# A gate table by expert, built by GpSimd's indirect adding DMAs into zeroed DRAM instead of by one-hot products on TensorE

## What is computed

```python
top_s, top_i = lax.top_k(sub_scores, K)                       # K = 16, 8 heads, 2 halves
cand_s = top_s[:, :, 0, :, None] + top_s[:, :, 1, None, :]
cand_id = top_i[:, :, 0, :, None] * N_KEYS + top_i[:, :, 1, None, :]
best_s, best_c = lax.top_k(cand_s.reshape(T, PEER_HEADS, K * K), K)
expert_id = jnp.take_along_axis(cand_id..., best_c, axis=-1)
gate = jax.nn.softmax(best_s, axis=-1)
a = jnp.einsum('pd,ped->pe', xb, expert_down[ids])
act = jax.nn.gelu(a, approximate=False) * gates
y = jnp.einsum('pe,ped->pd', act, expert_up[ids])
```

## Time and profile before

| | |
|---|---|
| median of 3 runs | 1516.51 us (1515.63 to 1518.48) |
| profiled execution, its own time | 1507.25 us |
| its span in the trace | 1505.4 us |
| busy: PE, DVE, ACT, POOL | 1386.3, 1022.5, 659.3, 50.7 us |
| mean granted clock of PE | 0.933 |

### The profile page before, as it was taken

One profiled execution on the slowest core, in us unless ns is written; L12 is line 12 of the kernel. 1 busy time (PEld: TensorE's weight loads), 2 busy tenths in 40 slices (PEclk: granted clock), 3 DMA queues, 4 the chain that ended last, 5 costly groups with the idle time before them and its releaser, 6 DMA issues.

```text
span 1505.4 us, 20658 instructions
## 1 busy us (share of the span) xinstructions
PE 1386.3 (92%) x8489; PEld 1235.0 (82%) x8489; DVE 1022.5 (68%) x1900; ACT 659.3 (44%) x853; POOL 50.7 (3%) x37
## 2 busy tenths in 40 slices
PE   2788987999999999999999999999799987799998
PEld 2576846999998999999888888888677976689987
DVE  5878746689999999844676676677646144545554
ACT  1445413454454444444545454454534144435443
POOL 0005000000000000000000000000001120000000
PEclk7788988999999999999999999999989555999999
DMA  9664444546655666768877887786535400425552
GB/s 365 229 223 148 150 151 157 187 176 236 240 194 214 249 252 252 277 259 330 301 275 279 292 290 288 269 315 235 189 126 184 141 1 1 167 101 180 198 194 84
DMA packets 118999, 316.05 MB, mean 210 GB/s; under 512 B 7662, under 2 KB 45807, under 8 KB 112506
## 3 DMA queue, kind: packets, MB, share of 16 engines
q1 hardware_dynamic: 105498, 263.35, 48.6%
q10 hardware_dynamic: 6912, 33.56, 5.6%
q0 software_dynamic: 6496, 17.84, 3.2%
HBM read 279.06 MB, written 34.60 MB: 208 GB/s over the span
## 4 chain that ended last, share of the span: by engine, by line
PE 82%; DVE 10%; DMA 3%; ACT 2%; issue 1%; SPq 1%; DVEq 0%; ACTq 0%
PE ps L621 10%; PE ps L620 10%; PE ps L619 10%; PE ps L607 10%; PE ps L609 9%; PE ps L608 9%; PE ps L816 4%; PE ps L597 3%; PE ps L599 3%; PE ps L598 3%; DVE w_lo L1376 2%; PE ps L866 2%; DMA arena<-in_ada_w 2%; PE ps L659 1%; PE ps L878 1%
## 5 line engine op out<-in xcount | busy, mean ns | idle before, releaser
L1376 DVE TENSOR_TENSOR w_lo<-wring,w_hi 128x1024 fp32r<-128x1024 f32 (+1 forms) x404 | 489.7, 1220 | 265.6 <-ACT w_hi L1017 264.1
L1017 ACT CAST w_hi<-wring 128x1024 fp32r<-128x1024 f32 (+1 forms) x404 | 420.3, 1045 | 389.0 <-PE ps L609 243.3
L607 PE MATMUL ps<-hT_hi,w_hi 128*128 128x256 f32 x1408 | 396.4, 282 | 15.3 <-DVE w_lo L1376 6.0
L608 PE MATMUL ps<-hT_lo,w_hi 128*128 128x256 f32 x1408 | 391.9, 278 | 0.0
L609 PE MATMUL ps<-hT_hi,w_lo 128*128 128x256 f32 x1408 | 391.7, 278 | 0.0
L607 PEld LDWEIGHTS ps<-hT_hi,w_hi 128*128 128x128 f32 x1408 | 266.8, 189 | 17.7 <-DVE hT_lo L1399 5.5
L608 PEld LDWEIGHTS ps<-hT_lo,w_hi 128*128 128x128 f32 x1408 | 267.1, 190 | 0.3
L609 PEld LDWEIGHTS ps<-hT_hi,w_lo 128*128 128x128 f32 x1408 | 266.9, 190 | 0.0
L621 PE MATMUL ps<-w_hi,a_lo 128*128 128x512 f32 x640 | 252.2, 394 | 0.0
L620 PE MATMUL ps<-w_lo,a_hi 128*128 128x512 f32 x640 | 250.9, 392 | 0.0
L619 PE MATMUL ps<-w_hi,a_hi 128*128 128x512 f32 x640 | 248.3, 388 | 0.0
(11 more groups left out here) (286 smaller groups left out, 1311.7 us busy)
## 6 DMA issues: line engine op xcount, KB each, us to landing
wring<-in_peer_down SPq DMA_DIRECT2D x32, 2048.0 KB, 8.6
wring<-in_peer_up SPq DMA_DIRECT2D x32, 2048.0 KB, 7.7
wring<-in_w_in SPq DMA_DIRECT2D x12, 2048.0 KB, 7.8
pages<-in_ada_w POOLq DMA_DIRECT2D x8, 2048.0 KB, 8.2
acts_by_expert<-pages ACTq DMA_DIRECT2D x32, 512.0 KB, 2.7
peer_arena<-gates_by_expert SPq DMA_DIRECT2D x16, 1024.0 KB, 11.0
peer_arena<-acts_by_expert SPq DMA_DIRECT2D x32, 512.0 KB, 8.5
wring<-in_w_up SPq DMA_DIRECT2D x8, 2048.0 KB, 8.3
```

Source lines behind the costliest of these rows:

```text
L607: pe.matmul(o, hi[:, k, :], hT_hi[:, k, :], start=(k == 0), stop=False)
L608: pe.matmul(o, hi[:, k, :], hT_lo[:, k, :], start=False, stop=False)
L1017: act.copy(split_part(kind, w_hi, u, width(kind, j)), part_of(kind, wring[:, n % RING, :], u, width(kind, j))).then_inc(split_hi, 1)
L1376: dve.tensor_tensor(lo, part_of(kind, wring[:, n % RING, :], u, width(kind, j)), hi, ALU.subtract)\
```

## The change

The table in DRAM becomes one flat array of 16384 x 256 numbers, expert by token. ACT zeroes it early in the program, in 8 DMAs of 2 MB from a zeroed piece of SBUF: 2 behind the split of win R_V, 3 behind that of wout 0, 3 behind that of wout 1. DVE works out place and gate of each choice head by head, in place of one batch behind the last head, with 10 `w_lo` parts per head instead of 6. For each head, rank (16) and token block (2), POOL issues one indirect DMA, which adds 128 gates, one per token, to 128 places of the table: 256 DMAs. Before it starts a head it waits until the adds of the head before it, for the same block, have landed. The one-hot rows, the transposes, the products, ACT's copies of them and its stores fall away. SP waits at the same place as before, now for the adds. ACT's softmax exponential comes once per head, not once for all.

```diff
@@ DMA of SP
-                sp.dma_start(gates_in[:, turn % 2, :, :, :].rearrange("p g f t -> p g (f t)"),
-                             gates_dram[:, :, turn * 2 * EF * 16:(turn + 1) * 2 * EF * 16].rearrange("g p n -> p g n"))\
+                rows = gates_dram[turn * 2 * CHUNK * T:(turn + 1) * 2 * CHUNK * T, :]
+                sp.dma_start(gates_in[:, turn % 2, :, :], rows.rearrange("(f p t) one -> p f (t one)", p=P, t=T))\
                     .then_inc(gates_landed[turn % 2], 16)
...
-            for u in range(2):
-                sp.wait_ge(gates_stored[u], 16 * (T // 32))
+            for b in range(NB):
+                sp.wait_ge(gates_added[b], 16 * PK * PH)
@@ PE
-            pe.wait_ge(S["sel_ready"], NB)
-            for b in range(NB):
-                for k in range(3):
-                    mm = pe.transpose(ps[:, 4 + b, k * P:(k + 1) * P], sel[:, b, k, :], ident)
...
-                    if 0 <= turn < T // TT:
-                        spread_products(turn)
@@ ACT
+            def fill_gates(turns):
+
+                act.wait_ge(S["zero_ready"], 1)
+                n = NE * T // FILLS
+                for turn in turns:
+                    act.dma_start(gates_dram[turn * n:(turn + 1) * n, :].rearrange("(r p n) one -> p r (n one)", p=P, n=ZEROS),
+                                  zeros.unsqueeze(1).to_broadcast([P, n // (P * ZEROS), ZEROS])).then_inc(gates_zeroed, 16)
...
+            fill_gates(range(0, 2))
...
+            fill_gates(range(2, 5))
...
+            fill_gates(range(5, FILLS))
...
+            def gate_exp(head):
+
+                act.wait_ge(S["score_max"], head + 1)
+                act.activation(gate_of[:, :, head, :], gate_of[:, :, head, :], ACT.Exp).then_inc(S["exp_done"], 1)
@@ POOL
+            pool.wait_ge(gates_zeroed, 16 * FILLS)
+            for head in range(PH):
+                pool.wait_ge(S["sel_ready"], head + 1)
+                for b in range(NB):
+                    if head:
+                        pool.wait_ge(gates_added[b], 16 * PK * head)
+                    for k in range(PK):
+                        pool.indirect_dma_start(gates_dram, bass.IndirectOffsetOnAxis(ap=place_of[:, b, head, k:k + 1], axis=0),
+                                                gate_of[:, b, head, k:k + 1], None, compute_op=ALU.add)\
+                            .then_inc(gates_added[b], 16)
@@ DVE
+                    if half == 0:
+                        if head:
+                            finish_gates(head - 1)
+                        next_rest()
+                        if head:
+                            tell("sel_ready")
...
+                for half in range(2):
+                    both(lambda b: dve.tensor_tensor(pick[:, half, b], bestf[:, b, half, head, :].unsqueeze(2)
+                                                     .to_broadcast([P, PK, PK]),
+                                                     con("iota")[:, 0:PK].unsqueeze(1).to_broadcast([P, PK, PK]), ALU.is_equal))
...
-            for q in range(T // OT):
...
-                for t in range(OT):
-                    at = q * OT + t
-                    first, second, weight = (selT[:, k, at:at + 1] for k in range(3))
-                    dve.tensor_scalar(onehot[:, q % OB, 0, t, :], con("iota"), first, None, ALU.is_equal)
-                    ins = dve.tensor_scalar(onehot[:, q % OB, 1, t, :], con("iota"), second, weight, ALU.is_equal, ALU.mult)
```

More of the change, by code:

```diff
@@ L120, in constants @@
     parts["iota"] = np.tile(np.arange(NKEY), (P, 1))
+    parts["token"] = i[:, None]
     at, out = 0, []
@@ L298, in two_blocks @@
         acts_in = [peer_arena[:, 8192 + k * 1024:9216 + k * 1024].rearrange("p (f t) -> p f t", f=EF) for k in range(AHEAD)]
[L299 to L300 removed]
+        pick = peer_arena[:, 12288:13312].rearrange("p (k b i j) -> p k b i j", k=2, b=NB, j=PK)
+        zeros = arena[:, 16000:16000 + ZEROS]
         cand, cand2 = (h_flat[:, k * 512:(k + 1) * 512].rearrange("p (b n) -> p b n", b=NB) for k in range(2))
@@ L363, in two_blocks @@
         S = {n: sem(n) for n in names}
-        gates_stored = [sem(f"gates_stored{k}") for k in range(2)]
+        gates_zeroed = sem("gates_zeroed")
+        gates_added = [sem(f"gates_added{k}") for k in range(NB)]
         gates_landed = [sem(f"gates_landed{k}") for k in range(2)]
@@ L798, in _ @@
             key_scores(3)
-            for j in range(1, TURN_AFTER + 1):
+            for j in range(1, STEPS):
                 by_columns("dn", j)
-            pe.wait_ge(S["sel_ready"], NB)
-            for b in range(NB):
-                for k in range(3):
-                    mm = pe.transpose(ps[:, 4 + b, k * P:(k + 1) * P], sel[:, b, k, :], ident)
[L806 to L813, removed]
-                    for t in range(OT):
[L815 to L826, removed]
-                    if 0 <= turn < T // TT:
-                        spread_products(turn)
-            pe.wait_ge(S["spread_out"], T // TT)
             for j in range(STEPS):
@@ L1167, in _ @@
                         split("ex", 0, acts_in[0], parts=[u])
[L1168 to L1174, removed]
+                    part = SPLIT_BEFORE[NTH["dn", j]] + PARTS + u - SPLIT_BEFORE[NTH["wq", 3]]
+                    if part % RESTS == 1 and 1 <= part // RESTS <= PH:
+                        gate_exp(part // RESTS - 1)
                 down_gelu(j)
@@ L1670, in top16, with tell, finish_gates @@
                 next_rest()
+            def tell(name):
+                both.settle()
+                dve.sem_inc(S[name], 1)
+            def finish_gates(head):
+                dve.wait_ge(S["exp_done"], head + 1)
+                both(lambda b: dve.tensor_reduce(gsum[:, b, head:head + 1], gate_of[:, b, head, :], AX.X, ALU.add))
+                both(lambda b: dve.reciprocal(gsum[:, b, head:head + 1], gsum[:, b, head:head + 1]))
+                both(lambda b: dve.tensor_scalar(gate_of[:, b, head, :], gate_of[:, b, head, :],
+                                                 gsum[:, b, head:head + 1], None, ALU.mult))
             for head in range(PH):
@@ L1683, in _ @@
                       lambda b: besti[:, b, 0, head, :])
[L1685 to L1688, removed]
-                    .then_inc(S["score_max"], 1)
-            both(lambda b: dve.tensor_copy(topf[:, b], topi[:, b]))
-            both(lambda b: dve.tensor_scalar(besti[:, b, 1, :, :], besti[:, b, 0, :, :], 15, None, ALU.bitwise_and))
@@ L1703, in _ @@
-            dve.wait_ge(S["exp_done"], 1)
-            both(lambda b: dve.tensor_reduce(gsum[:, b, :], gate[b], AX.X, ALU.add))
-            both(lambda b: dve.reciprocal(gsum[:, b, :], gsum[:, b, :]))
-            both.settle()
-            for b in range(NB):
-                dve.tensor_tensor(gate[b], gate[b], gsum[:, b, :].unsqueeze(2).to_broadcast([P, PH, PK]), ALU.mult)\
-                    .then_inc(S["sel_ready"], 1)
-            for u in range(PARTS):
-                next_rest()
-            dve.wait_ge(S["sel_turned"], 1)
@@ L1727, in _ @@
-            dve.sem_inc(S["late_free"], 1)
+                both(lambda b: dve.tensor_tensor(gate_of[:, b, head, :], best[:, b, head, :],
+                                                 best[:, b, head, 0:1].to_broadcast([P, PK]), ALU.subtract))
+                both(lambda b: dve.tensor_scalar(besti[:, b, 1, head, :], besti[:, b, 0, head, :], 15, None, ALU.bitwise_and))
+                tell("score_max")
+                both(lambda b: dve.tensor_scalar(besti[:, b, 0, head, :], besti[:, b, 0, head, :], 4, None,
+                                                 ALU.logical_shift_right))
@@ L1728, in _ @@
+                next_rest()
+            finish_gates(PH - 1)
+            next_rest()
+            tell("sel_ready")
             for n in range(next(placed), SPLIT_BEFORE[NTH["ex", 0]]):
```

75 lines of the change are left out of this document (24 added, 51 removed).

## The result

The changed kernel takes 1718.73 us (median of 4 runs, 1716.59 to 1722.66) against 1516.72 us before (4 runs beside it): ratio 1.1334, 95% interval 1.1308 to 1.1359. It is 202 us slower. I had forecast 1458 us, and a range up to 1590.

A forecast was written before the change was run, and what follows sets the result against it. PE was taken to set the pace, with DVE almost full. From 1505.4 us of span, less 73.6 removed, plus 3 (DVE) and 12 (fills), came 1446.8; against the median, 1458 us, range 1444 to 1590.

The forecast's parts named there:

- the price of an add: POOL's time for one of 256 adds: taken as 1.0 us, bounds 0.53 and 3.68, nothing late up to 1.04 us.
- rival 2: POOL's queue of 256 DMAs, then SP before step 29: late by more than the gain, from 1.27 us per add; chance 0.32.
- the formula: POOL's lateness is 256 times the time of one add, less the 267 us POOL has; paid one for one.
- Removed: 73.6 us: PE in the dn stage: one-hot turns, transposes and a DVE holdup go, 73.6 us less, gelus every 10.88 us.
- DVE inside the heads: 3 us: DVE needs 27.5 to 29.1 us per head against PE's 27.2: 3 us late, range 0 to 10.
- The fills: 12 us: ACT issues 16 MB of fills, held 12 us per group of three: 7 plus 5 us late, range 3 to 22.
- Rival 3: POOL and DVE stop each other: adds' place reads hold DVE, 51 us at 0.2 us each, about 1509 us; chance 0.13.
- The rival's last sentence: DMA engines, 0.62 busy: the small adds could also slow the weight loads, at a price similar to rival 3's.

The follow-up runs named there:

- the run with 64 rows: Changed kernel with 64 partitions per add in place of 128, still 256 adds: 1701.74 us.
- fewer adds: Changed kernel with only ranks 0 to 3 of 16 added, 64 adds in place of 256: 1452.32 us; with fills also issued by POOL: 1437.09 us.
- before with fills: Kernel before with the eight fills added, issued by ACT at the same three places into memory nobody reads: 1527.78 us, ratio 1.0113.
- SP's wait moved: Changed kernel with SP's wait for the adds moved behind the weights of dn 29 to 31 and ex 0 and 1: 1684.66 us.
- the second mixed kernel: Mixed kernel (POOL adds tokens 128 to 255, PE products the rest) with SP's wait and gate loads ahead of the ex weights: 1480.21 us, ratio 0.9794.
- the first mixed one: Against the changed kernel, POOL adds only tokens 128 to 255, PE's one-hot products make the others, POOL issues 8 MB of fills: 1479.54 us, ratio 0.9809.

## Why the prediction was wrong

**The step that failed** is the price of an add: "with the places read I take 1.0 us. Then nothing is late." Measured are 2.11 us per add. The mechanism of rival 2 was right: POOL's queue, SP's wait ahead of step 29, PE still. So was the formula: 256 x 2.11 - 267 = 273 us late, and SP stood 271.2 us; 1458 + 273 = 1731 against 1718.7 measured. The stage lost 263.1 us by it, so some 8 us were hidden where I had 2. (Only the per-head wait for the adds before, which rival 2 also named, never showed: no gap between two adds is over 0.3 us.)

Where 2.11 comes from, in terms of my estimate of 1.0: an indirect write is 0.97 us, so issue and places were sized rightly. Left out were the adding (0.58), the gap between two rows (0.30), and the wait for DVE (0.25, the mean row of 1.80 less 1.55). I had taken the number of descriptors as the measure of nearness ("an eighth of the 2 MB load's"), and by the run with 64 rows all 128 make only some 0.28 us. The estimate from the price of small reads in the Trainium skill (GPSIMD Engine Reference, section 7, Performance pitfalls for Q7 kernels), 1.2 us, was nearer than mine, but it covers the reading of places alone, and the places cost 0.43 us.

**Removed: 73.6 us.** Right: steps of 10.87 us, mean 10.85.

**DVE inside the heads: 3 us.** It cost nothing; PE was busy in all of 340 to 640 us.

**The fills: 12 us.** The hold of 12 us per group was right (12.1 and 11.9), what it cost was not: 12.6 us up to the second group and 7.7 at it, where I had 7 and 5. The price by itself measures 12.5 us (fewer adds, fills on POOL or not) and 17 us (before with fills), both loosely; in the trace of the changed kernel it is up to 21.6, at the top of my 3 to 22. I had taken holding ACT and sharing the DMA engines as alternatives (12 or 3 us). Fills issued by POOL from 258 us on cost the first gelu nothing (321.58 us); whether those on ACT cost by the hold alone no run here shows.

**Rival 3** (POOL and DVE stop each other) exists with the roles changed: `w_lo` isn't lengthened, the adds are, by 0.86 us each beside a steady stream of parts. The Trainium skill (SBUF — State Buffer, section SBUF: two separate sides) says that the one that starts first has the pair for its whole instruction; by that rule an add behind a started `w_lo` waits for its end, the rows agree (601.76 us against 601.89). Without it the adds would take 256 x 1.86 = 476 us, still 209 too many. The rival's last sentence, that small adds slow the weight loads, came true for the direct writes, not for the adds.

**The range** ended at t = 1.56 us because I gave rival 2 only 0.32. The upper bound of 3.68 was in the rows, and 2.11 lies between; the range was too narrow for what the rows left open.

## What to carry to other kernels

Work moved to an idle engine as many small instructions has to be priced per instruction, gap included, and multiplied by their number before anything else: 256 x 2.11 us was more than the idle time of POOL. When the budget is too small for all, move what fits: half of the adds was worth 29 us, all of them cost 202. And ask of a cheaper form what it does to the streams beside it, since the next wall (for the direct writes the weight loads) may be near.

## What I had not expected of the hardware

- An indirect add of 128 elements took 1.55 us on POOL and one of 64 elements 1.41; the same write without adding 0.97, a direct write 0.54. Where nothing is waited for, 0.30 us lie between two indirect DMAs, whatever their kind. Beside DVE's two-input `w_lo` the add took 2.41 us, while direct writes kept their 0.54.
- Three 2 MB fills in rows of 1 KB held ACT for 13 us when it issued them. On POOL seven such issues took 1.15 us each, with a pause of 5.8 us behind the third, and the eighth came only 58.7 us after the seventh.
- Direct 0.5 KB writes to neighbouring places, some seven in 10 us, brought the weight loads from about 8 to 27 us; indirect ones, six in 10 us, left them as they were for 200 us.
- In some profiled executions PE fell to a slower pace at a granted clock of 1.00, busy throughout and with no wait in the trace: dn steps of 11.31 us in place of 10.88. It came behind step 15 or so with 64 adds (both kernels) and with SP's wait moved (256 adds), in the last seven steps of the second mixed kernel, and in the last three of the kernel before with fills. In three of these the ex steps were slower too (216 products in 50 us in place of 220). The changed kernel and the first mixed one don't show it. So it goes with no number of adds, and I have no explanation; it cost an execution some 7 us in the dn stage at most, so spans of single executions that differ by so little say nothing.
